# Experts in four classes by token count, and a 64-slot and a 32-slot round sharing one pass over the weights

## The reference

```python
logits = (hf @ w_router + b_router).astype(jnp.float32)
top_vals, top_idx = lax.top_k(logits, TOP_K)          # 4 of 32 experts for each token
gates = jax.nn.softmax(top_vals, axis=-1)
...
def expert_block(args):
    xb, e = args
    gu = xb @ w_gu[e] + b_gu[e]                        # 1024 -> 2048
    gate = jnp.minimum(gu[:, :D_EXPERT], SWIGLU_LIMIT)
    up = jnp.clip(gu[:, D_EXPERT:], -SWIGLU_LIMIT, SWIGLU_LIMIT)
    glu = gate * jax.nn.sigmoid(SWIGLU_ALPHA * gate)
    return ((up + 1.0) * glu) @ w_down[e] + b_down[e]  # 1024 -> 1024
```

## Time and profile before

| what | value |
|---|---|
| time, median of 3 runs | 2118.43 us (2117.85 to 2120.16) |
| span of the profiled execution | 2122.4 us |
| PE busy | 2027.5 us (96%) |
| DVE, ACT busy | 911.2 us (43%), 644.2 us (30%) |
| ring loads from HBM | 577.74 MB read, 273 GB/s over the span |
| expert loop in the trace | about 186 us to 1208 us |

### The profile page before, as it was taken

One profiled execution on the slowest core, in us unless ns is written; L12 is line 12 of the kernel. 1 busy time (PEld: TensorE's weight loads), 2 busy tenths in 40 slices (PEclk: granted clock), 3 DMA queues, 4 the chain that ended last, 5 costly groups with the idle time before them and its releaser, 6 DMA issues.

```text
span 2122.4 us, 32004 instructions
## 1 busy us (share of the span) xinstructions
PE 2027.5 (96%) x12406; PEld 1304.4 (61%) x12407; DVE 911.2 (43%) x1611; ACT 644.2 (30%) x981; POOL 56.2 (3%) x65
## 2 busy tenths in 40 slices
PE   6999999999999999999999999999999999999999
PEld 4864333433333323332343498979999999799999
DVE  2522122112222112221122365866885558776774
ACT  1422111111111111110111234553554354634653
POOL 0000000000000000000000121000000120000000
PEclk9997999999999999999999999999999999999999
DMA  9785999299999999999769953413665544234563
GB/s 347 276 325 243 412 417 417 118 417 417 419 418 417 417 419 418 417 417 418 287 257 418 366 159 117 157 64 100 199 214 164 164 140 145 82 120 159 172 196 110
DMA packets 222041, 580.37 MB, mean 273 GB/s; under 512 B 23520, under 2 KB 142048, under 8 KB 185984
## 3 DMA queue, kind: packets, MB, share of 16 engines
q1 hardware_dynamic: 221952, 579.09, 71.7%
HBM read 577.74 MB, written 1.31 MB: 273 GB/s over the span
## 4 chain that ended last, share of the span: by engine, by line
PE 71%; DMA 12%; SPq 8%; DVE 4%; ACT 3%; issue 2%; ACTq 0%; DVEq 0%
PE bank L1085 13%; DMA ring<-in_w_gu 9%; PE bank L1141 8%; SPq L685 4%; PE bank L1229 3%; SPq L687 3%; PE bank L812 3%; PE bank L1231 3%; PE bank L1230 3%; PE bank L1462 3%; PE bank L1464 3%; PE bank L1463 3%; PE bank L1037 3%; PE bank L1051 3%; PE bank L882 2%
## 5 line engine op out<-in xcount | busy, mean ns | idle before, releaser
L1085 PE MATMUL bank<-ring,heap 128*64 128x512 f32 x2176 | 491.6, 600 | 31.1 <-DMA ring<-in_w_gu 31.1
L1085 PEld LDWEIGHTS bank<-ring,heap 128*64 128x64 f32 x2176 | 148.3, 137 | 357.4 <-issue 262.7
L2091 DVE TENSOR_SCALAR heap<-bank 128x256 f32<-128x256 f32 (+1 forms) x72 | 26.7, 413 | 724.0 <-PE bank L1085 695.2
L1141 PE MATMUL bank<-ring,heap 128*64 128x512 f32 (+1 forms) x1152 | 255.1, 595 | 0.0
L1229 PE MATMUL bank<-h_hi,w_hi 128*128 128x256 f32 x640 | 185.7, 290 | 1.2 <-DVE w_lo L2177 1.2
L2372 DVE TENSOR_TENSOR w_lo<-ring,w_hi 128x2048 fp32r<-128x2048 f32 (+1 forms) x64 | 142.4, 2225 | 101.3 <-ACT w_hi L1785 101.3
L1462 PE MATMUL bank<-h_hi,w_hi 128*128 128x256 f32 x640 | 182.3, 285 | 3.4 <-DVE w_lo L2372 3.4
L1613 ACT ACT_TABLE_LOAD x32 | 41.1, 1283 | 470.3 <-DVE heap L2091 468.6
L1230 PE MATMUL bank<-h_lo,w_hi 128*128 128x256 f32 x640 | 182.8, 286 | 0.0
L1231 PE MATMUL bank<-h_hi,w_lo 128*128 128x256 f32 x640 | 182.8, 286 | 0.0
L1464 PE MATMUL bank<-h_hi,w_lo 128*128 128x256 f32 x640 | 181.8, 284 | 0.0
(11 more groups left out here) (350 smaller groups left out, 2987.4 us busy)
## 6 DMA issues: line engine op xcount, KB each, us to landing
ring<-in_w_gu SPq DMA_DIRECT2D x256, 1024.0 KB, 19.2
ring<-in_w_down SPq DMA_DIRECT2D x128, 1024.0 KB, 21.7
ring<-in_ffn_w_up SPq DMA_DIRECT2D x44, 1024.0 KB, 7.7
ring<-in_w_in SPq DMA_DIRECT2D x32, 1024.0 KB, 7.9
ring<-in_w_ada SPq DMA_DIRECT2D x24, 1024.0 KB, 10.5
ring<-in_ffn_w_down SPq DMA_DIRECT2D x16, 1024.0 KB, 5.2
ring<-in_w_out SPq DMA_DIRECT2D x8, 1024.0 KB, 5.0
ring<-in_w_in SPq DMA_DIRECT2D x3, 2048.0 KB, 26.7
```

What stands on the lines that cost most here:

```text
L1085: last = mm(psum[g][both[f], :], xgT[:, k % 4, k // 4, :], wt[:, g, :, :, f, :].rearrange("p i c n -> p (i c) n"), start=False, stop=k == ...
L1141: last = mm(psum[2][FEW * f:FEW * f + n, :], hidT[:, o:o + n], wt[:, 512 * f:512 * (f + 1)], start=k == 0, stop=k == DT - 1)
```

## The change

A fourth class is put in: up to 96 tokens take `passes(2)`, one **double** pass of 64 and 32 slots over the same chunks. The class of 160 becomes a single round followed by a double pass (before: 64, 64, 32 slots one after the other). The classes of 64 and 256 tokens are as before. The semaphore counts are kept in step by larger increments `u`.

A double pass walks the gate and up chunks once for both token groups: the wide products of chunk k go to banks 0 and 1, the 32-slot products of the same chunk to bank 2. The second group's tokens are gathered and transposed while the first chunks are worked on. Each chunk is released (`gu_used`, `dn_used`) after both have used it. The down products alternate the same way, 32 slots into bank 3 and 64 slots into bank 2. At its end a double pass combines the 32-slot result itself. Six more tiles of 256 columns or more hold the second group's values.

The core of the diff (the single round, the helpers and the ACT and DVE work of a single round are the old code, moved into functions):

```diff
-CLASSES = ((64, 1), (160, 3), (256, 4))
+CLASSES = ((64, 1), (96, 2), (160, 3), (256, 4))
...
-def turns(rounds):
-    marks = {1: (0, 4), 3: (0, 1, 2, 4), 4: (0, 1, 2, 3, 4)}[rounds]
-    return [(r, a, b - a) for r, (a, b) in enumerate(zip(marks, marks[1:]))]
+def passes(rounds):
+    marks = {1: ((0, 4),), 2: ((0, 2),), 3: ((0, 2), (2, 1)), 4: ((0, 1), (1, 1), (2, 1), (3, 1))}[rounds]
+    return [(r, at, u, rounds in (2, 3) and r == rounds - 2) for r, (at, u) in enumerate(marks)]
...
-        sgT = take_e(T)
+        sg_both = take_e(2 * T)
+        sgT, sgC = sg_both[:, 0:T], sg_both[:, T:2 * T]
+        xgC = take_e(4, 2, FEWER)
+        act_gc, act_uc, act_sc, hid_c, hidT_c = take_e(T), take_e(T), take_e(T), take_e(T), take_e(T)
+        y_c = take_e(512)
...
+            def gu_step(k, gate_done=None):
+                wt = gu_piece(k)
+                for g in range(2):
+                    for f in range(2):
+                        last = mm(psum[g][both[f], :], xgT[:, k % 4, k // 4, :],
+                                  wt[:, g, :, :, f, :].rearrange("p i c n -> p (i c) n"),
+                                  start=False, stop=k == DT - 1, skip_group_check=True)
+                    if k == DT - 1 and g == 0:
+                        last.then_inc(gate_full.sem, gate_done)
+                return last
+            def down_step(k, bank, x, o, n):
+                wt = piece(exp_stream, f"dn{k // 2}", 2)[:, k % 2, :]
+                for f in range(2):
+                    last = mm(psum[bank][FEW * f:FEW * f + n, :], x[:, o:o + n], wt[:, 512 * f:512 * (f + 1)],
+                              start=k == 0, stop=k == DT - 1)
+                return last
...
+            def gu_few(k, gate_done=None):
+                wt = gu_piece(k)
+                for g in range(2):
+                    for f in range(2):
+                        for c in range(2):
+                            last = mm(psum[2][quarter[2 * f + c], T * g:T * (g + 1)], xgC[:, k % 4, k // 4, :],
+                                      wt[:, g, :, c, f, :], start=False, stop=k == DT - 1, skip_group_check=True)
+                    if k == DT - 1 and g == 0:
+                        last.then_inc(gate_full.sem, gate_done)
...
+            def double(e, r, at, u):
+                to = at + u
+                pe.wait_ge(xT_ready.sem, xT_ready.at(R + at, e))
+                if r == 0:
+                    pe.wait_ge(sel_ready.sem, sel_ready.at(1, e))
+                biases()
+                def wide(k):
+                    if r == 0:
+                        gu_arrived(e, k)
+                    return gu_step(k, u)
+                def few(ks):
+                    for k in ks:
+                        last = gu_few(k, u)
+                        if k < DT - 1:
+                            last.then_inc(gu_used.sem, 1)
+                    return last
+                wide(0)
+                pe.wait_ge(y_ready.sem, y_ready.at(R + at, e))
+                gather(r + 1).then_inc(x_full.sem, u)
+                wide(1)
+                pe.wait_ge(x_ready.sem, x_ready.at(R + to, e))
+                turn_gathered(3).then_inc(xT_full.sem, u)
+                wide(2)
+                pe.wait_ge(xT_ready.sem, xT_ready.at(R + to, e))
+                biases_few()
+                few((0, 1, 2))
+                for k in range(3, DT - 2):
+                    wide(k)
+                    few((k,))
+                wide(DT - 2)
+                wide(DT - 1).then_inc(up_full.sem, u)
+                few((DT - 2, DT - 1)).then_inc(up_full.sem, u)
+                pe.wait_ge(sg_ready.sem, sg_ready.at(R + at, e))
+                combine(y_sb, sgT).then_inc(combined.sem, u)
+                if r == 0:
+                    pe.wait_ge(pickg_ready.sem, pickg_ready.at(1, e))
+                turn_gates(r, 0)
+                turn_gates(r + 1, T).then_inc(sg_full.sem, 2 * u)
+                pe.wait_ge(g_ready.sem, g_ready.at(2 * to, e))
+                pe.wait_ge(pick_ready.sem, pick_ready.at(2, e))
+                gather(0, 0).then_inc(x_full.sem, u)
+                pe.wait_ge(sg_ready.sem, sg_ready.at(R + at + 2 * u, e))
+                for h in range(2):
+                    if h == 1:
+                        pe.wait_ge(up_taken.sem, up_taken.at(to, e))
+                    pe.wait_ge(hid_ready.sem, hid_ready.at(2 * at + (h + 1) * u, e))
+                    turn_hidden(3 if h == 0 else 1, hid, (2 * h, 2 * h + 1)).then_inc(hidT_full.sem, u)
+                pe.wait_ge(up_taken.sem, up_taken.at(to + u, e))
+                pe.wait_ge(hid_ready.sem, hid_ready.at(2 * (to + u), e))
+                turn_hidden(2, hid_c, (0, 1)).then_inc(hidT_full.sem, 2 * u)
+                pe.wait_ge(x_ready.sem, x_ready.at(R + at + 2 * u, e))
+                turn_gathered().then_inc(xT_full.sem, u)
+                pe.wait_ge(hidT_ready.sem, hidT_ready.at(2 * (to + u), e))
+                for j in range(4):
+                    if r == 0:
+                        pe.wait_ge(exp_in[f"dn{j}"].sem, exp_in[f"dn{j}"].at(16, e))
+                    for k in (2 * j, 2 * j + 1):
+                        last = down_step(k, 3, hidT_c, few_at(k), FEWER)
+                    if j == 3:
+                        last.then_inc(y_full.sem, u)
+                    for k in (2 * j, 2 * j + 1):
+                        last = down_step(k, 2, hidT, down_at(k), FEW)
+                    last.then_inc(*((dn_used.sem, 1) if j < 3 else (y_full.sem, u)))
+                pe.wait_ge(y_ready.sem, y_ready.at(R + to, e))
+                combine(y_c, sgC).then_inc(combined.sem, u)
             def expert(e, rounds):
-                for r, at, u in turns(rounds):
-                    final = r == rounds - 1
-                    few = final and rounds == 3
...
+            def double(e, at, u):
+                to = at + u
+                gathered(R + to, e, 2).then_inc(x_ready.sem, u)
+                act.wait_ge(xT_full.sem, xT_full.at(R + to, e))
+                f(xgC.rearrange("p a b c -> p (a b) c"), psum[3].rearrange("p (q s) -> p q s", s=FEW)[:, :, 0:FEWER], ACT.Copy) \
+                    .then_inc(xT_ready.sem, u)
+                gated(at, u, e)
+                act.wait_ge(g_ready.sem, g_ready.at(2 * (to + u), e))
+                f(act_sc, act_gc, ACT.Sigmoid, scale=ALPHA).then_inc(sig_ready.sem, 2 * u)
+                act.wait_ge(combined.sem, combined.at(to, e))
+                act.wait_ge(sg_full.sem, sg_full.at(to + u, e))
+                f(sg_both, psum[3], ACT.Copy).then_inc(sg_ready.sem, 2 * u)
+                gathered(R + to + u, e, 0).then_inc(x_ready.sem, u)
+                next_input(R + to + u, u, e)
+                act.wait_ge(y_full.sem, y_full.at(to, e))
+                f(y_c, psum[3], ACT.Copy).then_inc(y_ready.sem, u)
+                act.wait_ge(y_full.sem, y_full.at(to + u, e))
+                f(y_sb, psum[2], ACT.Copy).then_inc(y_ready.sem, u)
...
+            def double(e, at, u):
+                to = at + u
+                dve.wait_ge(x_full.sem, x_full.at(R + to, e))
+                select(e + 1).then_inc(pick_ready.sem, 1)
+                wide_hidden(at, u, e)
+                dve.wait_ge(up_full.sem, up_full.at(to + u, e))
+                v.tensor_scalar(act_gc, psum[2][:, 0:T], LIMIT, None, ALU.min).then_inc(g_ready.sem, 2 * u)
+                v.tensor_scalar(act_uc, psum[2][:, T:2 * T], LIMIT, -LIMIT, ALU.min, ALU.max).then_inc(up_taken.sem, u)
+                dve.wait_ge(g_ready.sem, g_ready.at(2 * (to + u), e))
+                dve.wait_ge(up_taken.sem, up_taken.at(to + u, e))
+                v.scalar_tensor_tensor(out=act_uc, in0=act_uc, scalar=1.0, in1=act_gc, op0=ALU.add, op1=ALU.mult) \
+                    .then_inc(e_chain.sem, 3 * u)
+                dve.wait_ge(e_chain.sem, e_chain.at(3 * (to + u), e))
+                dve.wait_ge(sig_ready.sem, sig_ready.at(2 * (to + u), e))
+                v.tensor_tensor(hid_c, act_uc, act_sc, ALU.mult).then_inc(hid_ready.sem, 2 * u)
+                for h in range(2):
+                    hidden_part(h, at, u, e)
+                dve.wait_ge(hidT_full.sem, hidT_full.at(2 * (to + u), e))
+                v.tensor_copy(hidT_c, psum[2][:, 0:T]).then_inc(hidT_ready.sem, 2 * u)
```

More of the change, by code:

```diff
@@ L1031, in acc_of, with gather @@
                 return psum[4 + 2 * f + c // 2][:, T * (c % 2):T * (c % 2) + T]
-            def gather(r):
+            def gather(r, bank=2):
                 for t in range(TT):
                     for f in range(2):
-                        last = mm(psum[2][both[f], :], pick[:, t, FEW * r:FEW * (r + 1)], htok[:, t, 512 * f:512 * (f + 1)],
-                                  start=t == 0, stop=t == TT - 1)
+                        last = mm(psum[bank][both[f], :], pick[:, t, FEW * r:FEW * (r + 1)],
+                                  htok[:, t, 512 * f:512 * (f + 1)], start=t == 0, stop=t == TT - 1)
@@ new lines, in turn_gates, with turn_hidden, gu_piece @@
```

(36 more changed lines are left out.)

235 lines of the change are left out of this document (113 added, 122 removed).

## The result

The changed kernel takes 2104.12 us (median of 4 runs, 2098.71 to 2108.34), the kernel before 2119.3 us in the same comparison (2117.85 to 2121.85); the ratio is 0.9919, with a 95% interval of 0.9902 to 0.9937. By the medians it is 15.2 us faster (by the ratio 17) where 23.6 us were forecast, and its median lies 2.1 us above the range and 9.3 above the forecast. The span of the profiled execution is 2103.6 us (its own time 2105.42), 18.8 us shorter than the 2122.4 us of before.

The account below looks back on a forecast made before the run. The weight queue was taken to bound the kernel between about experts 11 and 27, PE elsewhere. Gains of 28.4 (expert 27) + 1.7 (expert 6) - 6.5 (jumps) = 23.6 us gave 2094.8 us from the 2118.43 median, range 2085 to 2102.

Parts of the forecast that it names:

- What bounds the kernel: Expert loop: PE bounds up to about expert 11 and from 28 to 31, the weight queue in between.
- The length of a double pass: Double pass: 49.4 us, 1.7 more than the two rounds it replaces, with 2.1 for changes of array shape.
- Expert 27: Expert with 75 tokens: one double pass replaces three rounds, so expert 28 starts 28.4 us earlier, its weights in time.
- Expert 6: Expert with 146 tokens: PE takes 1.7 us longer, but the queue reaches expert 8 earlier, gaining 1.7 us.
- Jumps in PE's program: One new code-fetch stall of 3.24 us before expert 6 and one after expert 27, 6.5 us lost.
- Behind the loop: After the expert loop: work is released by PE and merely moves with it, so the gain carries through.
- Rival 3: Longer program no longer stays at hand, returns to loop's head stall: 2118, or 2210 with slow clock; chance 0.06.
- Rivals 2 and 4: 2: dearer double passes or slow clock after stalls, 2101.2 or 2105, chance 0.2; 4: transfers behind expert 27, 2105, chance 0.03.
- edits at nothing: Double pass: extra DVE and ACT steps, second gather's copies and moved DMA issue are covered, costing nothing.

Follow-up runs that it names:

- grouped kernel: Changed kernel with each double pass's products grouped by shape, wide ones and 32-slot ones apart; 2103.2 us, ratio 0.9913 to the kernel before.
- e4: Kernel before without its never-run block for experts of more than 160 tokens; 2122.0 us, ratio 1.0007 to the kernel before.
- e1: Changed kernel without the never-run block for experts of more than 160 tokens; 2091.7 us, ratio 0.9867 to the kernel before.
- e9: Changed kernel without the block for more than 160 tokens and with double-pass products grouped by shape; 2091.2 us, ratio 0.9861 to the kernel before.
- e6: Changed kernel without the block for more than 160 tokens, blocks in the order 64, 160, 96; 2097.4 us, ratio 0.9896 to the kernel before.
- e7: Changed kernel, all four classes, with the block for more than 160 tokens first in the loop; 2125.2 us, ratio 1.0025 to the kernel before.
- e8: Kernel before with the shared double pass but no class of 96 (classes 64, 160, 256); 2118.7 us, ratio 0.9995 to the kernel before.
- e11: Kernel before with a second copy of the three-round block in PE's program alone, taken by expert 27; 2137.6 us, ratio 1.0087 to the kernel before.
- e2: Kernel before with only the class of 96 added, as two successive rounds without the shared pass; 2245.7 us, ratio 1.059 to the kernel before.
- e10: Changed kernel with one never-run block more in VectorE's program alone; 2238.6 us, ratio 1.0547 to the kernel before.

## Why the prediction missed

The median lies 9.3 us above the forecast of 2094.8. The profiled spans account for 4.8 of it: 2.0 in the loop, at expert 6, and 2.8 behind it. The other 4.5 us are no term of the sum. The span of before lay 3.97 us above its median, that of the changed kernel 0.52 below; as the profiled execution of the changed kernel took 1.8 us more than its span, that of before took an estimated 2124.2 us, above all four runs of before. A change read from it looks larger than the medians give.

- **What bounds the kernel** held: the queue sets the pace up to expert 27, PE behind it.
- **The length of a double pass**: 49.4 us forecast, 49.28 measured, and the 0.16 us for a change of shape was 0.14. By the Trainium skill (TensorEngine Tiling (Array Packing), Key Properties) a change of tiling mode drains the engine; the trace agrees in that each change costs 0.14 us, though it doesn't show what the time goes to.
- **Expert 27**: 28.4 us forecast, 28.5 measured. Its weights and those behind it were in time.
- **Expert 6**: the mechanism held (the queue starts expert 8 when PE frees the first chunk), the size did not, since PE came 11.0 us later.
- **Jumps in PE's program** is the step that failed, a term of the sum with the wrong sizes and places. I took the gap after expert 6 as given (3.24 us) and added one gap of 3.24 us before expert 6 and one after expert 27. Measured: 5.1 us up to the start of expert 6's double pass (3.66 idle, 0.55 and 1.1 for a slow clock, less an earlier start of 0.25), 4.75 us more than before after expert 6, and none after expert 27. The terms at expert 6 and of the jumps together were -1.7 + 6.5 = +4.8 us; they are +6.8: expert 7 was to start 1.7 + 3.24 = 4.9 us later and started 11.0 later. A stall doesn't cost a fixed 3.24 us. With 792 and 864 products the gaps at a return are 7 to 14.8 us, with 3 to 5 packets of the instruction queue in each, where those of 3.6 us hold one; so I read the long ones as several fetches in a row.
- **Behind the loop** I expected a mere shift ("what comes behind is released by PE and moves with it"); it was 2.8 us longer, more than the loop's own miss. It is 917.0 us in the changed and the grouped kernel, 914.1 and 914.5 in before and e4, 911.6 and 912.8 in e1 and e9, and 910.3 to 911.3 in e6, e7, e8 and e11, so it doesn't follow the size of PE's loop. Stretches of slow clock lie at different places in before and in the changed kernel. Whether the code's place in memory does this was not tried, and stays open.
- **Rival 3**, the longer program that no longer stays at hand, is real and lay close, but on VectorE, where I had not looked: e2 and e10 are 5.5 to 5.9% slower than before. The changed kernel escapes it by fewer than 16 rows of VectorE's program, if e2 and it differ in nothing else that matters. The sum under this rival was off as well: 30.1 us of gain less 36 us of stalls is 2124, not 2118.
- **Rivals 2 and 4** named times nearer to the measured one (2101.2 and 2105), but not for what happened: the slow clock of rival 2 came behind one new stall and not two, with 1.65 us and not 3.2, the passes weren't dearer, and nothing waited for chunks behind expert 27.
- Of the edits at nothing, the shorter steps of DVE and ACT were covered: apart from 0.4 us in all at the first down products, PE waits for neither more than before.

How VectorE's longer program slows the weights themselves isn't settled: in e10 PE waits for chunks and not for VectorE, and the weight queue is busy 91.2% of the time, where it was 101.8% in the changed kernel. That the length of VectorE's program causes it is shown, and that fetches come with it in every expert; by which way they slow the queue is not.

## What to carry to other kernels

In a hardware loop with branches, count the instructions of every engine's whole loop, also those that never run: the new class paid 28.5 us at its expert, code that is never executed took some 12 us back, and a block more on another engine made it a loss of 5%. Before working from a profiled execution, compare its span with the runs. When two forms of a pass are interleaved, count the changes of array shape (0.14 us each here). Freeing a buffer earlier helps only until the consumer is itself what the next transfer waits for.

## What the runs showed of the hardware

- TensorE's loop code: with 324 products no gap after the long expert, with 504 none or 3.1 to 3.5 us, with 612 3.0 to 3.2, with 792 7.0 to 11.1, with 864 11.05. Between experts 0 and 1 every kernel has a gap, also that of 324 products, of 3.1 to 3.5 us (12.22 in e7). A product is up to four instructions in the trace (64 MATMUL and as many LDWEIGHTS for the 32 products of a gate and up part; a transpose is two), so I estimate 504 products at 1900 instructions and 612 at 2300, waits not counted. The Trainium skill (Runtime: NRT & Kernel Launch, Instruction fetch mechanics) gives PE room for 2048 instructions; the runs fit this size, since the gap comes and goes at 504 and is always there from 612 on, but they don't measure it. The same section says that a taken branch out of the current window of two pages forces a fetch before execution goes on; here the trace disagrees: the loop's head is returned to some 28 times without a gap.
- VectorE: with 217 rows of its program in the loop (the changed kernel) there are no fetches from 600 to 1000 us, with 233 (e2) and 299 (e10) some five in every expert, and these two kernels are 124 and 118 us slower than before. The rows were counted in the program; no view of the profile shows them.
- A gap of 3 us on PE is at times followed by the lower clock level, at times not: after 214.66 us expert 1's products took 13.88 us (granted clock 1.00 of full, the upper of its two levels, 2.4 GHz), in the changed kernel after a gap of 3.44 us they took 16.35 (0.85 on the mean, so part of the time at the lower level, 1.2 GHz).
